# One launch order, one scaling and a list of vector steps moved in a two-block transformer kernel

## What is computed

```python
# first block, layer 0 (stick-breaking attention) and layer 1 (dilated attention)
u = rms_norm(h, g_mix_pre[i])              # h / sqrt(mean(h*h)+eps) * gain
q, k, v = split(u @ w_in_sb)               # layer 0: 16 heads of 64
z = (q @ k^T) * 64**-0.5
a = exp(log_sigmoid(z) + sum of the later log_sigmoid(-z)), where key < query
h = h + rms_norm((a @ v) @ w_out_sb, g_mix_post[0])
# layer 1: for each of 3 groups q, k are turned by cos and sin of positions * freq
h = h + rms_norm(relu(rms_norm(h, g_ffn_pre) @ w_ff_in)**2 @ w_ff_out, g_ffn_post)
h = h + (p[i] @ w_ple[i]) * sigmoid(rms_norm(h, g_ple[i]) @ w_ple_gate[i])
# second block, per layer i: six shift/scale/gate vectors for tokens and for context
ml = silu(c) @ w_mod[i] + b_mod[i];  mc = silu(c_ctx) @ w_mod[i] + b_mod[i]
```

## Time and profile before

| | |
|---|---|
| three runs | 1702.23, 1702.30, 1706.57 us; median 1702.3 |
| profiled execution | 1700.7 us, its span 1698.8 us |
| PE busy | 1648.4 us, 97% of the span |
| DVE busy | 1204.1 us, 71% |
| ACT busy | 914.3 us, 54% |

### The profile page before, as it was taken

The page is one execution under the profiler, slowest core; times in us unless marked ns, Lnnn a source line. Parts: engine busy times, 40 slices in busy tenths (PEclk is TensorE's granted clock), DMA queues, the critical chain, the costliest instruction groups (busy, mean ns, idle before and its releaser), DMA issues.

```text
span 1698.8 us, 25392 instructions
## 1 busy us (share of the span) xinstructions
PE 1648.4 (97%) x10062; PEld 1413.4 (83%) x10062; DVE 1204.1 (71%) x1412; ACT 914.3 (54%) x1185; POOL 0.2 (0%) x4
## 2 busy tenths in 40 slices
PE   7999999999998999999999999999999999999998
PEld 6988888988887888899865778888888878789998
DVE  5866778778885878766578478876667666577754
ACT  5777664475337765467367453332234265565553
POOL 0000000000000000000000000000000000000000
PEclk9999999999999999999999999999999999999999
DMA  6834668745651566633130325456644432145652
GB/s 225 264 115 132 197 196 274 237 149 188 213 172 51 156 198 226 208 125 116 53 124 2 124 84 181 144 162 228 216 140 154 165 108 85 49 150 176 194 174 80
DMA packets 242824, 264.71 MB, mean 156 GB/s; under 512 B 7055, under 2 KB 223122, under 8 KB 242706
## 3 DMA queue, kind: packets, MB, share of 16 engines
q1 hardware_dynamic: 240780, 258.77, 47.0%
q10 hardware_dynamic: 1926, 4.32, 0.7%
HBM read 262.01 MB, written 1.05 MB: 155 GB/s over the span
## 4 chain that ended last, share of the span: by engine, by line
PE 78%; DVE 11%; ACT 8%; issue 2%; DMA 0%; ACTq 0%; DVEq 0%
PE ps L788 77%; DVE wlo L2107 3%; DVE y L2438 2%; ACT pr L2022 1%; ACT whi L1410 1%; DVE u L2545 1%; DVE pr L2727 1%; DVE y L2556 1%; PE ps L1303 1%; DVE qk L2290 0%; DVE qk L2288 0%; DVE work L2285 0%; ACT u L1619 0%; DVE small L2719 0%; ACT y L1885 0%
## 5 line engine op out<-in xcount | busy, mean ns | idle before, releaser
L788 PE MATMUL ps<-u,whi 128*128 128x256 f32 (+1 forms) x3544 | 872.6, 333 | 11.8 <-DVE u L2594 5.5
L788 PEld LDWEIGHTS ps<-u,whi 128*128 128x128 f32 x3544 | 599.2, 190 | 97.4 <-issue 14.0
L788 PE MATMUL ps<-u,wlo 128*128 128x256 f32 (+1 forms) x2052 | 629.0, 307 | 0.0
L2107 DVE TENSOR_TENSOR wlo<-raw,whi 128x2048 fp32r<-128x2048 f32 (+6 forms) x213 | 454.1, 2132 | 185.0 <-ACT whi L1410 175.8
L1410 ACT ACTIVATE whi<-raw 128x2048 fp32r<-128x2048 f32 (+6 forms) x213 | 381.0, 1789 | 195.4 <-PE ps L788 172.8
L788 PEld LDWEIGHTS ps<-u,wlo 128*128 128x128 f32 x2052 | 388.8, 189 | 19.5
L788 PE MATMUL ps<-hid,whi 128*128 128x512 f32 (+1 forms) x1212 | 352.7, 363 | 0.0
L788 PE MATMUL ps<-hid,wlo 128*128 128x256 f32 (+1 forms) x864 | 260.9, 302 | 0.0
L788 PEld LDWEIGHTS ps<-hid,whi 128*128 128x128 f32 x1212 | 216.2, 189 | 39.7 <-issue 3.4
L788 PEld LDWEIGHTS ps<-hid,wlo 128*128 128x128 f32 x864 | 163.1, 189 | 7.0
L2438 DVE SCALAR_TENSOR_TENSOR y<-idle_half,cc,y 128x1024 f32<-128x1024 f32 x70 | 89.9, 1285 | 5.0
(11 more groups left out here) (281 smaller groups left out, 1650.5 us busy)
## 6 DMA issues: line engine op xcount, KB each, us to landing
raw<-in_ffn_w_up SPq DMA_DIRECT2D x44, 1024.0 KB, 5.1
raw<-in_w_ff_in SPq DMA_DIRECT2D x32, 1024.0 KB, 5.4
raw<-in_w_ff_out SPq DMA_DIRECT2D x32, 1024.0 KB, 5.5
modw<-in_w_mod SPq DMA_DIRECT2D x112, 256.0 KB, 4.1
idle_half<-in_w_mod SPq DMA_DIRECT2D x80, 256.0 KB, 3.9
raw<-in_w_in_dil SPq DMA_DIRECT2D x18, 1024.0 KB, 5.2
raw<-in_w_in_sb SPq DMA_DIRECT2D x11, 1024.0 KB, 8.1
raw<-in_w_ple_gate SPq DMA_DIRECT2D x8, 1024.0 KB, 5.2
```

The lines of the kernel that those rows point to most:

```text
L788: return pe.matmul(out_, lhsT, rhs, start=start, stop=stop, skip_group_check=True)
L2107: nc.vector.tensor_tensor(wlo[:, s % SPLIT, 0:n], raw[:, c["r"] % RAW, 0:n], whi[:, s % SPLIT, 0:n].bitcast(F32), ALU.subtract).then_inc(* ...
```

## The change

**Launch.** Only the identity and ones (128 KB) are loaded ahead of the first weights; the other constants, frequencies and positions follow chunks 1 and 2. PE transposes the first 16 rows of gains, waits for `x`, and transposes it into four banks that stay untouched. ACT forms `uh` straight from PSUM with the gain, DVE forms `ul`, without the root. The splits of chunks 0 and 1 are woven in. `h` is copied out of PSUM by DVE, behind the low part of chunk 1. The squares, their sums and the root run beside `stick_v`; the two extra matmuls are gone. The root is applied where the projections are read out: per token on the values by ACT (`root_columns`), and by DVE on the queries and keys (`stick_scaled`, in place of ACT's copy). The context is transposed behind chunk 3.

**Sines.** DVE forms the arguments behind the low part of chunk 4, ahead of `conditioning`; ACT takes the sines behind the second group of `ff_out0` (chunk 40).

**Conditioning steps.** They are dealt out singly. Per chunk now: 2 in 1, 2, 4 and 5; 1 in 13 to 15; 1 in 18 to 22 and 24 to 32 (`ff_in0`); in `ff_out0` 2 in 33 to 35, 1 in 36, 2 in 38 to 44; 1 in 58, 59, 64 and 65; 1 in 76 to 89 and in 91 (`ff_in1`); in `ff_out1` 2 in 92 to 98, 1 in 99. From the second block on the list is the same. The folding of the first set moves from chunk 13 to 24, the second from 42 to 38, the third from 60 to 61, the fourth from 72 to 91. PE has a new wait for the last stored set ahead of the last dilated values.

**Rotation.** In the dilated phase DVE turns the group before ahead of the split instead of behind it.

```diff
-        share = dict(stick_qk=1, stick_v=2, stick_out=1, ff_out0=2, dil_qk0=1, dil_v0=1, dil_qk1=1, dil_v1=1,
-                     dil_qk2=1, ff_out1=2, up00=4, down00=4, up01=4, down01=4)
+        share = dict(stick_v=2, stick_qk=2, stick_out=1, ff_in0=1, ff_out0=2, dil_v0=1, dil_v1=1, ff_in1=1, ff_out1=2, up00=4, down00=4, up01=4, down01=4)
...
-        todo = [(st, c, k) for st in sets for c in range(st["c0"], st["c1"], 2) for k in range(KD)]
+        todo = [(st, c, k, v) for st in sets for c in range(st["c0"], st["c1"], 2) for k in range(KD) for v in st["vecs"]]
...
-            if job["name"] == "stick_qk" and ck["g"] < 2:
+            if job["name"] == "ff_in0" and ck["g"] == 0 or job["name"] == "stick_v" and r > 2 or job["name"] == "stick_qk" and ck["g"] > 1:
...
# PE
+                            if not c["first"]:
+                                square_sums(1, 0)
+                                square_sums(1, 1)
...
+                            if c["first"]:
+                                square_sums(1, 2)
+                                square_sums(1, 3)
+                            else:
+                                pe.wait_ge(*at("moved", "rows"))
+                                root_turned(1)
...
-                    pe.wait_ge(*at("group_read_s", ("group", phases[stick_i - 2]["groups"][j + 1][0]["gi"])))
+                    pe.wait_ge(*at("group_read_v", ("group", phases[stick_i - 2]["groups"][j + 1][0]["gi"])))
...
-                    for b in (6, 7):
-                        mm(ps[:, b, :], ones, squares[:, 0:4, :].rearrange("p j c -> p (j c)"), True, True)
...
# ACT, launch
+                    for k in range(KD):
+                        if k == 4:
+                            split_high(0)
+                        act.wait_ge(*at("turned", ("x", k // 2)))
+                        act.wait_ge(*own())
+                        nc.scalar.activation(uh[:, k, 0:S], launch_tile(k), ACT.Copy, scale=gain(phases[2], k)).then_inc(
+                            *up("operand_high", (2, k)))
+                    split_high(1)
+                    for g in range(4):
...
+                        nc.scalar.activation(sq[:, g % 2, :].rearrange("p (t c) -> p t c", t=2), h[:, 2 * g:2 * g + 2, 0:S], ACT.Square).then_inc(*up("stat_squares", (1, g)))
+                        if g == 1:
+                            split_high(2)
+                            split_high(3)
+                            split_high(4)
...
+                        if p["name"] == "ff_out0" and grp[0]["g"] == 1:
+                            angles()
...
# DVE, launch
+                    for k in range(KD):
+                        if k == 4:
+                            split_low(0)
+                        dve.wait_ge(*at("operand_high", (2, k // 2 * 2 + 1)))
                         dve.wait_ge(*own())
+                        nc.vector.scalar_tensor_tensor(ul[:, k, 0:S], launch_tile(k), gain(phases[2], k), uh[:, k, 0:S].bitcast(F32), ALU.mult, ALU.subtract).then_inc(
+                            *up("operand_low", (2, k)))
+                    split_low(1)
+                    for g in range(4):
+                        dve.wait_ge(*own())
+                        nc.vector.tensor_copy(h[:, 2 * g:2 * g + 2, 0:S], ps[:, (6, 7, 3, 2)[g], :].rearrange("p (k c) -> p k c", k=2)).then_inc(
+                            *up("normed", ("x", g)))
+                    split_low(2)
...
# DVE, queries and keys
+            def stick_scaled(p, g):
+
+                c = p["groups"][g][0]
+                dve.wait_ge(*at("weights_used", c["s"]))
+                dve.wait_ge(*own())
+                nc.vector.scalar_tensor_tensor(
+                    (k1 if g % 2 else q1)[:, g // 2 * 2:g // 2 * 2 + 2, :], acc(c, S), 1.0 if g % 2 else HD ** -0.5, root_wide(2), ALU.mult, ALU.mult).then_inc(
+                    *up("group_read_v", ("group", c["gi"])))
...
+                    if g >= 1:
+                        stick_scaled(p, g - 1)
                     if g >= 3:
                         stick_mask(2 * g - 6)
                         stick_mask(2 * g - 5)
...
# DVE, loop over the groups of a linear phase
+                        if p["evac"] == "qk2" and (p["name"] != "dil_qk0" or g > 1):
+                            rotate_pending()
                         if grp[-1]["s"] + SPLIT not in early + late + behind_tail(p):
                             split_low(grp[-1]["s"] + SPLIT)
+                        if grp[-1]["r"] == 1:
+                            angles()
+                            conditioning()
                         mod_keep(grp[-1]["r"] - 3)
```

More of the change, by code:

```diff
@@ L145, in build @@
         mod_landed = [ctx.enter_context(nc.semaphore(f"mod_landed{i}")) for i in range(5)]
-        loaded = {n: ctx.enter_context(nc.semaphore(f"loaded_{n}")) for n in ("squares", "rows", "more_rows", "freq", "pos", "x", "ctx", "arena", "p")}
+        loaded = {n: ctx.enter_context(nc.semaphore(f"loaded_{n}")) for n in ("ident", "gain", "squares", "rows", "more_rows", "freq", "pos", "x", "ctx", "arena", "p")}
         stored = ctx.enter_context(nc.semaphore("stored"))
@@ L1653, in evac @@
                 elif kind == "qk1":
-                    act.wait_ge(*own())
-                    nc.scalar.activation((k1 if g % 2 else q1)[:, g // 2 * 2:g // 2 * 2 + 2, :], A_, ACT.Copy, scale=1.0 if g % 2 else HD ** -0.5).then_inc(
-                        *up("group_read_s", key))
+                    pass
                 elif kind == "qk2":
@@ new lines, in _ @@
+                    nc.scalar.activation(vec[:, 0:16], ps[:, 0, 0:16], ACT.Copy).then_inc(*up("moved", "gain"))
+                    for k in range(KD):
+                        if k == 4:
+                            split_high(0)
+                        act.wait_ge(*at("turned", ("x", k // 2)))
+                        act.wait_ge(*own())
+                        nc.scalar.activation(uh[:, k, 0:S], launch_tile(k), ACT.Copy, scale=gain(phases[2], k)).then_inc(
+                            *up("operand_high", (2, k)))
@@ new lines, in _ @@
+                    act.wait_ge(*at("turned", "rows"))
+                    act.wait_ge(*own())
+                    nc.scalar.activation(vec[:, 16:at_row], ps[:, 5, S + 16:S + at_row], ACT.Copy).then_inc(*up("moved", "rows"))
+                    act.wait_ge(*at("stat_summed", (1, 3)))
+                    act.wait_ge(*own())
+                    nc.scalar.activation(lnv[:, 0:S], ps[:, 4, 0:S], ACT.Ln, scale=1.0 / D, bias=small[:, 40:41]).then_inc(*up("scalar_step"))
+                    act.wait_ge(*own())
@@ L1845, in _ @@
+                    nc.scalar.activation(rstd[:, 0:S], lnv[:, 0:S], ACT.Exp, scale=-0.5).then_inc(*up("rstd_ready", 1))
+                elif i in (1, 2):
+                    pass
                 elif kind == "stats":
@@ L1847, in _ @@
                     s0 = p.get("s0", 0)
-                    for k in range(4 if i == 1 else p["n"]):
+                    for k in range(p["n"]):
                         if k >= 2:
@@ L1868, in _ @@
                         *up("rstd_ready", i))
-                    if i == 1:
-                        act.wait_ge(*at("turned", "rows"))
-                        act.wait_ge(*own())
-                        nc.scalar.activation(vec[:, 0:at_row], ps[:, 0, 0:at_row], ACT.Copy).then_inc(*up("moved", "rows"))
                 elif kind == "apply":
@@ L1889, in _ @@
                             *up("operand_high", (i, k)))
-                    if i == 2:
-                        for s in range(1, SPLIT):
-                            split_high(s)
                 elif kind == "linear":
@@ L1901, in _ @@
                         if p["name"] == "dil_qk0" and grp[0]["g"] == 2:
-                            act.wait_ge(*at("turned", (p["sums"], "root")))
-                            act.wait_ge(*own())
-                            nc.scalar.activation(small[:, 48:50], ps[:, 5, 0:2 * P].rearrange("p (t c) -> p t c", t=2)[:, :, 0], ACT.Copy).then_inc(
-                                *up("turned_copied", (p["sums"], "root")))
+                            root_columns(p["sums"])
                         if p.get("stat") and grp[0]["g"] >= 1:
@@ L1933, in _ @@
                             heads[0] += 1
+                        if p["name"] == "ff_out0" and grp[0]["g"] == 1:
+                            angles()
                         mod_rows(grp[-1]["r"] - 1)
-                        if p["name"] == "stick_v":
-                            context_copied(2 * grp[0]["g"] + 1)
-                        if not already and grp[-1]["s"] + SPLIT not in early + late:
+                        if p["name"] == "stick_v" and grp[0]["g"] == 1:
+                            for q in (2, 3, 0, 1):
+                                context_copied(q)
+                        if not already and grp[-1]["s"] + SPLIT not in early + late and grp[-1]["s"] > 1:
                             split_high(grp[-1]["s"] + SPLIT)
@@ L2508, in _ @@
[L2508 to L2513 removed]
```

(7 more changed lines are left out.)

231 lines of the change are left out of this document (119 added, 112 removed).

## The result

The changed kernel took 1708.6 us (median of 7 executions, 1707.1 to 1709.8) against 1702.3 us for the one before (median of 7, 1700.3 to 1706.6), measured side by side: ratio 1.0034, 95% interval 1.0024 to 1.0045. A second comparison gave 1.0023 (1.0014 to 1.0032; 11 executions against 15). So it is slower by 4 to 6 us, at the mark of 0.3% that separates a difference from none. The forecast was 1703, with 1709 as upper end of the range: the first comparison lies 0.4 us inside it. The profiled execution took 1707.09 us, 6.4 us more than the one before (1700.7).

A forecast was written before the change was run, and what follows sets the result against it. PE was taken as the bound, busy 1648.4 of 1698.8 us. Terms +0.6 - 4.1 + 4.3 = +0.8 gave 1701.5 us on the profiled execution; the forecast was 1703 as runs' median lies 1.6 above, range 1697.5 to 1709.

The forecast's parts named there:

- the narrower range of 1699 to 1707: Whole kernel: the forecast's own range, within 4 us of 1703, given a chance of 0.5.
- Launch, +0.6: Launch to first scores: PE's 5.8 us lead is lost to DVE's list; scores at 58.2 against 57.62 us.
- what I had put in: Chunk 0 in the launch: 3.6 us at half clock after PE idles, costing 1.8 us; DVE then idles nearly 5 us.
- Scores to `ff_in0`, 0: From the scores on: PE runs without a wait as before; zero, between -0.5 and +0.5 us.
- the rival of the half clock: Chunk 0 and scores: half clock comes twice, +2.7, total 1705.8 us; chance 0.17 together with the dilated exchange.
- Sines on ACT, 0: Behind chunk 40: 3.4 us more on ACT, covered by the split's 11.1 us; zero, up to 3.4 without cover.
- Dilated, -4.1: Dilated projections: without steps DVE needs 4.7 us per period, so PE's three waits go; -2 to -4.5 us.
- The exchange that I named as a rival: Dilated part: something else takes over PE's waits, 2 us less gain, 1705 us; chance 0.17 together with half clock twice.
- Feed-forward inputs, +4.3: `ff_in0` and `ff_in1`: steps make DVE's period 6.02 against PE's 5.54 us; 0.9 and 3.4 us, between 0 and +13.6.
- the reserve of 4.0 us: Feed-forward inputs: how far DVE can fall behind before PE waits for the bank, delaying PE from group 10 in `ff_in1`.
- two last waits: `ff_in0`: chunk 23 without a step and the fold behind chunk 24 leave only these waits, 0.9 us.
- The rival on the other side: Feed-forward inputs: DVE bounds them at once, +13.6 in place of +4.3, total 1712.4 us; chance 0.13.

The follow-up runs named there:

- the kernel before with the fitted list: The kernel before with only the rebalanced list of steps, made to fit each stage's room; launch, sines and scaling as before: 0.9984, 1700.3 us.
- the run with the old list: The changed kernel with the list of steps of the kernel before, none in the feed-forward inputs: 0.9990, 1701.56 against 1703.3 us.
- the second trace: The changed kernel run once more, unaltered: ratio 1.0023 against the kernel before, span 1706.3 us.
- the last two kernels: The changed kernel with the rebalanced list, sine arguments ahead of chunk 4's low part (repeat) or behind it: 0.9957 and 0.9960, 1696.1 and 1696.0 us.

## Why the prediction was right, and where not

The time fell inside the range, if close to its upper end (and 1.6 us outside the narrower range of 1699 to 1707), and the mechanisms that the forecast named are the ones found, but its size was off: +6.4 us in the profiled execution against +0.8, and 4 to 6 us in the medians. By its steps:

- **Launch, +0.6: measured -0.5.** "The launch changes nothing" held, and so did the reason, the list on DVE: waits of 1.65 and 4.01 us where 2.2 and 4.3 were forecast. The way there was partly wrong. "The two extra matmuls that kept PE at work are gone" is true of these two only; fourteen more stand in the same row of the timeline of before (18.23 us below) and stay, and with them chunk 0 ran at full clock. The run without them shows what I had put in: the half clock, at 2.6 us and not 1.8, and DVE idle for 5.06 us ahead of the low part of chunk 4. In the changed kernel DVE idled 2.62 us there, not 5, and began that part at 27.95 us in place of the 30.2 of the sum. Of these 2.3 us 1.1 reached the scores (57.09 against 58.2); the rest went into the items behind, which took 0.8 us more than I had up to the low part of chunk 6 and 0.4 more from there on. The row that I read as two matmuls and a gap:

```profile
18.23 4.91 PE L788 MATMUL ps<-squares 128*128 128x512 f32 x18
```
- **Scores to `ff_in0`, 0: measured +1.0** beside the fold. This is half of the rival of the half clock. In all five traces with the wait of 4.0 us ahead of the scores the clock was 0.50 behind it, and the way to the wait at about 124 us took 1.0 to 2.0 us longer than before; in none of the eight traces without that wait was the clock 0.50 there. The first 30 products from the scores on took 5.08 us in the changed kernel and 3.58 in the eight: the half clock costs 1.5 us (2.2 to 2.5 where it lasted longer), of which a part is made up behind it, since PE then waits less. The +1.0 rests on 1.6 us for the fold that is gone; the kernel before with the fitted list, which has neither that fold nor the half clock there, is 1.4 us shorter in this stretch, so it may be 0.8. The rule cited in the forecast, from the Trainium skill, "TensorE: Matmul & The Clock Gate", Part 1, that idle stretches take the fast clock back, agrees with these runs. I had given it to a rival and left it out of the sum.
- **Sines on ACT, 0.** In the run with the old list the stretch that holds them is 2.47 us longer, 2.44 of it by cadence. Right.
- **Dilated, -4.1: measured -3.2, and +1.1 given back behind it.** The waits for DVE went. The exchange that I named as a rival, with 2 us, is what happened: 1.16 us of waiting for "the copies of the values", then 0.61 for DVE in the softmax.
- **Feed-forward inputs, +4.3: steps +4.9** (1.8 and 3.1, forecast 0.9 and 3.4; 3.9 in the second trace). DVE's period of 6.02 us was measured as 6.11, and PE's chunks stretched from the tenth on, as the reserve of 4.0 us had it. In `ff_in0` I had two last waits of about 0.45; they were 0.29 and 0.96, and 0.6 us I can't place. The folds, which I took as moved at no cost, cost 0.6 us more where they now stand.
- **Not in the sum:** cadence +2.9, half clock at 498 us -1.5 and at 1471 us +1.4. The two half clocks are chance as far as the runs show, and so is the cadence of `ff_in0`, since before by itself falls either way in each. In `ff_in1` both traces of before are fast and both of the changed kernel slow in part, one by 0.8 us more than the other; its fold and waits stand there, and the cadence changes at such places, so a part of it may belong to the change.

Without the last item the change does -0.5 + 1.0 - 3.2 + 1.1 + 4.9 + 0.6 - 0.2 = +3.7 us, against +0.8 (the -0.2 is the stretch to 1465 us). The dilated term failed most, by 2 us with what came behind it; the clock, the steps and the folds failed to the same side, and two of these four (the dilated exchange, the clock behind the new wait) stood in my own list of rivals. The rival on the other side, DVE as the bound of the feed-forward inputs at once, did not come: the reserve was there. That the median came out at the edge of the range and not beyond it is in part luck, since chance alone moved one trace of before by 2.7 us.

## What to carry to other kernels

Work that is spread over an engine's idle time has a room in every stage: the stage's period less the engine's own work in it. Laid out by that room its steps cost nothing that the runs could show, beside the folds; a list that spares one stage by overfilling three others loses what it gained. An earlier start is worth what the next engine's list lets through: the same launch was worth 0.5 us with four pairs of steps ahead of the scores, 3.4 with three, and 6.2 with two. And a difference of a few microseconds between two single traces has to be cleared of what two traces of one kernel already differ by.

## What the runs showed of the hardware

- TensorE's products had two cadences at full granted clock, 346 to 347 and 353 ns for a pair of 512 and 256 columns, 1.9% apart. The Trainium skill, "TensorE: Matmul & The Clock Gate", section "Wait — 56ns, not 53.3ns?", gives one fixed cost per matmul at the fast clock, about 2.5 ns. The rows here don't agree: 768 columns at 2.4 GHz are 320 ns, which leaves 13 ns per product in the one cadence and 17 in the other. The switch between them came only at stalls and folds.
- The half clock behind a wait of PE: in 6 of 6 cases where PE was idle for 4.0 to 4.3 us (five at the scores, one in the launch), in 8 of 13 behind the 2.1 us at about 1470 us, in 1 of 4 behind the 2.2 us in the launch of the kernels with the old one, in 1 of 2 behind the 1.77 us at the dilated scores, in 9 of 13 at about 900 us behind two waits of 1.0 and 1.4 us, and in none of 13 behind the 1.6 to 1.8 us at about 380 us. So a wait of about 2 us costs its own length and sometimes 1.3 to 1.5 us more. Near 900 us the half clock cost nothing when it lasted 3.4 us (703.70 us for the stretch with it and 703.69 without, the last two kernels) and 1.6 to 1.8 us when it lasted 6.8 us.
- Fourteen products that nothing reads, over 3.2 of the 4.3 us between the transposes and chunk 0, go with a chunk 0 at full clock in all eight traces that have them there; in the one without them its first part ran at 0.50, and the time was 4 us longer (1711.1 against 1707.2 us).
